# The first block of a two-block fp32 network on one core: a depthwise convolution accumulated in PSUM banks, VectorE's order within an attention step, a layer norm in five pieces, and two gate chunks spread over three steps

## The reference

```
h = rmsnorm(x, norm_g);  proj = h @ w_in            # (512, 1024) @ (1024, 3584)
y_a = silu(layernorm(depthwise_conv31(a_u * sigmoid(a_v)) + b)) * silu(a_z)
y_b = b_b * depthwise_conv3(b_c * b_x) * silu(b_z)
y_c = window_gqa(rope(c_q), rope(c_k), c_v, sink) * silu(c_z)     # 4 heads, band of 128
y_d = neighborhood_attn(d_q, d_k, d_v, bias) * silu(d_z)          # 4 heads, 8 x 64 grid
x = x + concat(y_a, y_b, y_c, y_d) @ w_out
```

## Time and profile before

| | us |
|---|---|
| median of 3 | 2107.06 (2106.79 to 2108.96) |
| the profiled execution | 2103.85 |
| its span in the profile | 2102.0 |
| granted TensorE clock over the span | 0.973 of full |
| first block, layers 0 and 1 | about 0 to 318 and 318 to 612 |

### The profile page before, as it was taken

The page is one execution under the profiler, slowest core; times in us unless marked ns, Lnnn a source line. Parts: engine busy times, 40 slices in busy tenths (PEclk is TensorE's granted clock), DMA queues, the critical chain, the costliest instruction groups (busy, mean ns, idle before and its releaser), DMA issues.

```text
span 2102.0 us, 25400 instructions
## 1 busy us (share of the span) xinstructions
PE 1970.2 (94%) x9140; PEld 1627.9 (77%) x9140; DVE 1184.4 (56%) x2109; ACT 745.4 (35%) x1079; POOL 1041.1 (50%) x1299
## 2 busy tenths in 40 slices
PE   6789799899789999899989999999998999999997
PEld 5677678677678888788878888778886888888886
DVE  7886658876566666646433233756666453332335
ACT  3333434334332545432413223324554224132230
POOL 5434245434264345556546464643446565574653
PEclk9899999999899999999999999999999999999998
DMA  4112122112122122222222222222212222222221
GB/s 168 67 67 71 61 74 97 62 65 81 33 78 95 66 81 81 80 100 82 105 80 101 100 96 88 98 80 81 81 61 94 89 99 100 94 89 98 100 101 60
DMA packets 28049, 178.85 MB, mean 85 GB/s; under 512 B 3872, under 2 KB 4000, under 8 KB 7456
## 3 DMA queue, kind: packets, MB, share of 16 engines
q1 hardware_dynamic: 24192, 169.88, 22.6%
q10 hardware_dynamic: 3744, 7.45, 1.1%
HBM read 175.22 MB, written 2.10 MB: 84 GB/s over the span
## 4 chain that ended last, share of the span: by engine, by line
issue 41%; POOL 35%; PE 23%; DVE 0%; POOLq 0%; DVEq 0%; ACT 0%
POOL W_lo L476 35%; PE bank L496 22%; DVE X L1945 0%; POOLq L480 0%; PE bank L544 0%; POOLq L473 0%; PE bank L537 0%; POOL SPARES L467 0%; DVE TMP L1507 0%; DVE PRE L1590 0%; DVE PR L1593 0%; DVE X L2315 0%; DVE PR L2312 0%; DVEq L169 0%; POOLq L476 0%
## 5 line engine op out<-in xcount | busy, mean ns | idle before, releaser
L476 POOL TENSOR_TENSOR W_lo<-W_raw,W_hi 128x256 fp32r<-128x256 f32 x1280 | 1039.3, 850 | 1024.3 <-ACT W_hi L1045 1024.0
L496 PE MATMUL bank<-H_hi,W_hi 128*128 128x512 f32 x1280 | 511.7, 400 | 13.4 <-POOL W_lo L476 11.0
L496 PE MATMUL bank<-H_hi,W_lo 128*128 128x512 f32 x1280 | 503.3, 393 | 0.0
L496 PE MATMUL bank<-H_lo,W_hi 128*128 128x512 f32 x1280 | 502.5, 393 | 0.0
L496 PE MATMUL bank<-Y_hi,W_hi 128*128 128x512 f32 x964 | 386.1, 401 | 22.2 <-POOL W_lo L476 11.4
L496 PE MATMUL bank<-Y_lo,W_hi 128*128 128x512 f32 x964 | 381.2, 395 | 0.0
L496 PE MATMUL bank<-Y_hi,W_lo 128*128 128x512 f32 x964 | 380.6, 395 | 0.0
L1045 ACT ACTIVATE W_hi<-W_raw 128x2048 fp32r<-128x2048 f32 x160 | 305.1, 1907 | 197.1 <-DMA W_raw<-in_stream 196.7
L496 PEld LDWEIGHTS bank<-H_hi,W_hi 128*128 128x128 f32 x1280 | 243.4, 190 | 68.0 <-POOL W_lo L476 15.4
L496 PEld LDWEIGHTS bank<-H_hi,W_lo 128*128 128x128 f32 x1280 | 242.8, 190 | 52.3
L496 PEld LDWEIGHTS bank<-H_lo,W_hi 128*128 128x128 f32 x1280 | 243.7, 190 | 48.6
...
## 6 DMA issues: line engine op xcount, KB each, us to landing
...
```

Of the source, the lines that this page charges most:

```text
L476: ins = nc.gpsimd.tensor_tensor(W[1][:, s, part], W_raw[:, s, part], W[0][:, s, part].bitcast(F32), ALU.subtract)
L496: mm = pe.matmul(out, lhs[a], rhs[b], start=(not begun and k == 0 and a == 0 and b == 0), stop=(not more and k == n - 1 and a == 1), skip_ ...
```

## The change

Four edits, all in the first block:

1. `conv_a` does channel tile 0 first and then tile 1, accumulating in a PSUM bank (`OB`, then `NB`); the last tap writes to `CA`. A tap waits for the tap just before. `FIRST_TAPS` becomes 6, 4, 7, 6, 2 and a new 6 ahead of `values(0)`, so that tile 0 is complete before attend(0) needs `OB`; steps 1 to 7 take the 31 taps of tile 1, in three places of each step.
2. VectorE's order in a step: `PT_lo` and the maximum come first, `lo_y(i-1)` after the maximum, and y(i) before the filler chunk's products (but in step 0). ScalarE takes the high part of y(i) before that of the merged gate, and waits for a freed bank before the next tanh rather than after its own.
3. The layer norm starts one step later (`LN_STEP` 7) and is cut into pieces that stand at three places of steps 8 to 12 (`norm_step`); its sum of squares on TensorE comes after attend(9), its spread in step 10, and the tanh goes into `HA` rather than `TMP`.
4. az0 and az1 are computed in steps 11, 12 and 13 (5, 3 + 2 and 6 k-tiles, `PARTS`), and o00 does k-tiles 0 and 1 last of its part.

```diff
-LN_STEP = 6
+LN_STEP = 7
 FILL = {0: "dz0", 1: "dz1", 2: "bc0", 3: "bc1", 4: "bx0", 5: "bx1", 6: "bb0", 7: "bb1",
-        8: "cz1", 9: "bz0", 10: "bz1", 11: "az0", 12: "az1", 14: "o00", 15: "o01"}
+        8: "cz1", 9: "bz0", 10: "bz1", 12: "az0", 13: "az1", 14: "o00", 15: "o01"}
+PARTS = {11: (("az0", 0, 5),), 12: (("az0", 5, 8), ("az1", 0, 2)), 13: (("az1", 2, 8),)}
-FIRST_TAPS = (15, 5, 6, 5, 2)
-TAPS = {0: 5, 1: 5, 2: 6, 3: 6, 4: 3, 5: 2, 6: 2}
+FIRST_TAPS = (6, 4, 7, 6, 2, 6)
+TAPS = {1: (1, 3, 2), 2: (1, 3, 2), 3: (1, 3, 2), 4: (1, 1, 1), 5: (1, 1, 1), 6: (1, 3, 1), 7: (1, 1, 0)}
...
+                for piece in PARTS.get(i, ()):
+                    part(*piece)
+                if i in FILL and i not in PARTS:
                     chunk(FILL[i])
...
-            taps = iter([(j, c) for j in range(CONV_A) for c in range(2)])
+            taps = iter([(j, c) for c in range(2) for j in range(CONV_A)])
...
+                    acc = (OB, NB)[c][:, :]
+                    dve.wait_ge(*own.last(0))
                     if j == 0:
-                        dve.wait_ge(*own.last(1))
-                        nc.vector.tensor_scalar(CA[:, c, :], src, w, par("conv_a_b", c), ALU.mult, ALU.add) \
-                            .then_inc(dve_step, own.step())
+                        ins = nc.vector.tensor_scalar(acc, src, w, par("conv_a_b", c), ALU.mult, ALU.add)
                     else:
-                        dve.wait_ge(*own.last(1))
-                        nc.vector.scalar_tensor_tensor(CA[:, c, :], src, w, CA[:, c, :], ALU.mult, ALU.add) \
-                            .then_inc(dve_step, own.step())
+                        ins = nc.vector.scalar_tensor_tensor(acc if j < CONV_A - 1 else CA[:, c, :], src, w, acc,
+                                                             ALU.mult, ALU.add)
+                    ins.then_inc(dve_step, own.step())
...
+            conv_a(FIRST_TAPS[5])
             values(0)
+            def norm_step(i, turn):
+                if (i, turn) == (LN_STEP + 1, "end"):
+                    dve.wait_ge(b1.ss.sem, b1.ss.at(l, "mean"))
...
+                elif (i, turn) == (LN_STEP + 2, "exp"):
...
+                elif (i, turn) == (LN_STEP + 2, "probs"):
...
+                elif (i, turn) == (LN_STEP + 3, "exp"):
+                    diagonals(b1, l, "var", spread=False)
+                elif (i, turn) in ((LN_STEP + 3, "end"), (LN_STEP + 4, "exp")):
+                    c = i - (LN_STEP + 3)
+                    dve.wait_ge(b1.bc.sem, b1.bc.at(l, "var"))
...
+                elif i == LN_STEP + 5 and turn != "end":
+                    c = ("exp", "probs").index(turn)
+                    dve.wait_ge(b1.aux.sem, b1.aux.at(l, f"ln{c}"))
...
             for i in range(2 * STEPS):
-                if i:
-                    lo_y(i - 1)
...
-                n_taps = TAPS.get(i, 0)
+                n_taps = TAPS.get(i, (0, 0, 0))
                 if i % STEPS < STEPS - 1:
                     softmax_max(i + 1)
-                    conv_a(n_taps // 4)
-                    n_taps -= n_taps // 4
+                if i % STEPS:
+                    lo_y(i - 1)
+                conv_a(n_taps[0])
+                norm_step(i, "exp")
+                if i % STEPS < STEPS - 1:
                     softmax_rest(i + 1)
-                conv_a(n_taps)
+                conv_a(n_taps[1])
+                norm_step(i, "probs")
...
                 nc.vector.scalar_tensor_tensor(PRE[r, i % 2, 0:256], OB[of:of + HD, 0:256], 0.5, ZB[r, h // 2,
                                                half * 256:(half + 1) * 256], ALU.mult, ALU.mult) \
                     .then_inc(b1.pre.sem, own.event(b1.pre, l, f"y{i}"))
...
+                if i in FILL and i:
+                    chunk(FILL[i])
+                norm_step(i, "end")
+                if i != LN_STEP:
+                    conv_a(n_taps[2])
```

More of the change, by code:

```diff
@@ L136, in b1_splits @@
         if i == STEPS:
-            out += ["cq0", "cq1", "ck0", "ck1", "cv"]
+            out += [f"y{i - 1}"] * low + ["cq0", "cq1", "ck0", "ck1", "cv"]
         if i == 1:
@@ L140, in b1_splits @@
         out += [f"pt{i}a"] if i < STEPS else [f"pt{i}a", f"pt{i}b"]
+        if low and i % STEPS:
+            out.append(f"y{i - 1}")
+        if not low:
+            out.append(f"y{i}")
         fill = FILL.get(i, "")
-        if i == LN_STEP + 4:
-            out.append("y" + FILL[i - 1])
-        if fill[:2] in ("bz", "az") and i != LN_STEP + 3:
+        if fill[:2] in ("bz", "az"):
             out.append("y" + fill)
-        out.append(f"y{i}")
-    return out
+    return out + [f"y{2 * STEPS - 1}"] * low
 def filled(name):
@@ L672, in chunk, with part @@
                 mm.then_inc(b1.done.sem, 1)
+            def part(name, first, last):
+                n = B1_CHUNKS.index(name)
+                k, c = divmod(n, 2)
+                if first == 0:
+                    if c == 0:
+                        begin_unit(1, l, k)
+                    free_bank(n)
+                pairs = chunk_pairs(slot_of(1, l, k), c, NORMED)[first:last]
+                mm = three(pe, b1_bank(name)[:, :], pairs, begun=first > 0, more=last < KT)
+                if last == KT:
+                    mm.then_inc(b1.done.sem, 1)
             def scores(i):
@@ L1128, in begin, with chunk @@
                 prep(1, l, k)
-            def chunk(name, begun=False):
+            def chunk(name, begun=False, last=True):
                 if not begun:
@@ L1150, in chunk @@
                 elif kind in ("dz", "cz", "bz", "az"):
+                    if name in ("dz1", "cz0", "cz1", "bz0"):
+                        act.wait_ge(b1.free.sem, b1.free.at(l, {"dz1": "dz0", "cz0": "dz1", "cz1": "cz0",
+                                                                "bz0": "cz1"}[name]))
                     act.wait_ge(*own.last(1))
```

124 lines of the change are left out of this document (54 added, 70 removed).

## The result

The changed kernel takes **2070.8 us** (median of 4, 2069.5 to 2071.8) against 2106.9 for the kernel before (median of 4, 2105.9 to 2109.0): a ratio of 0.983 with a 95% interval of 0.981 to 0.984, so 36.2 us won. The forecast was 2067.4, with a range of 2055 to 2085. Sign and range held; the terms of the sum did not all hold, and the errors went both ways.

A forecast was written before the change was run, and what follows sets the result against it. TensorE, busy 94%, was taken as the bound, its waits largely on a late VectorE. Terms of 49.7 us less 10 for the clock took 2103.85 to 2064.2, plus 3.2 for the median: 2067.4, range 2055 to 2085.

The forecast's parts named there:

- First attend: Up to the first attend: earlier split of dk1 cuts TensorE's wait; 11.3 us won in layer 0, 8.4 in layer 1.
- The price of the new tap: VectorE's convolution tap on a PSUM bank: 0.78 us whatever GpSimd does, bounds 0.68 and 1.37.
- Steps 0 to 7: Neighbourhood attention: VectorE still sets the stretch, 61.8 us instead of 71.3, 9.5 won in each layer.
- Between: Projections between the attention halves: from 1.9 us lost to 1.4 won, taken as 0.
- Last stretch: Window attention, steps 9 to 15: 65.2 us instead of 70.2 and 71.2, 5.0 and 6.0 won.
- the charge for the clock: Half-clock loss set against the gains: 4 us per last stretch, 1 per stretch of steps 0 to 7, 10 in all.
- The new stall at the spread: Step 10: the norm's diagonals come at 10.6 us after attend(9), TensorE wants them at 7.2; a 3.4 us stall.
- A: Whole program as summed: 2067.4 us, own range 2058 to 2077; chance 0.56.
- Rival D: Taps on a bank are still held up by GpSimd at 1.08 us: 15 us less won, 2083; chance 0.08.
- E: Slower than before: a tap reading and writing the same bank takes 1.37 us, 2137 in all; chance 0.04.
- C: Stalls too short to bring the clock down: 50 us won, 2057; chance 0.09.
- B: Five-piece norm costs more, step 10's stall drops the clock, the final stretch wins nothing: 2078 us; chance 0.20.

The follow-up runs named there:

- e1: Changed kernel with the convolution's accumulator back in SBUF, a tap still waiting for the one just before: 2078.7 us.
- e2: Kernel before with only the places of the taps changed (6, 4, 7, 6, 2 and 6 ahead, 31 in steps 1 to 6): 2101.4 us.
- e4: Changed kernel with 29 of the 31 taps of each channel tile left out, so the convolution is not computed: 2046.2 us.
- e3: Changed kernel with az0 and az1 whole in steps 12 and 13 and none in step 11: 2071.2 us.
- e7: Changed kernel with the next step's row maximum ahead of PT_lo in steps 8 to 14: 2059.7 us.
- e9: Changed kernel with the row maximum ahead of PT_lo in steps 8 to 14 and the merged gate's split a step later: 2052.8 us.
- e5: Changed kernel with the low half of y ahead of PT_lo again from the second step on: 2075.1 us.

## Why the prediction was right, and where it was not

**First attend: right.** 11.3 and 8.4 won by the forecast, 9.9 and 8.1 measured. dk1's split ended at 75.7 for 74.9 forecast (the taps began 0.5 us later than I took), and the wait ahead of the first scores was 1.6 for 1.2; layer 1 has none. The price of the new tap, 0.78, was exact. That VectorE's serial wait and not the bank makes it 0.78 and not 0.69 is shown by e1's and e2's rows with GpSimd idle. The price of the old tap I had read wrongly at its lower end: of the 13 taps in 12.09 us the last ones ran with GpSimd idle (it works from 57.7 to 66.4 there), so 0.92 is a mix of 0.69 and some 1.1, and not a tap beside GpSimd.

**Steps 0 to 7: the mis-sized term.** 9.5 won a layer by the forecast (8.5 with the clock), 4.2 and 4.3 measured. I took each step as the longer of VectorE's list and TensorE's 8.05 us. In step 5 my 9.2 us for VectorE was about right, as its rows in the changed kernel show: `PT_lo` starts at 136.47 and the next at 146.20, 9.7 us apart. The step takes 12.1 on TensorE, from attend(5) at 137.21 to attend(6) at 149.33.

```profile
136.47 0.68 DVE L1504 TENSOR_TENSOR PT_lo<-bank,PT_hi 128x512 fp32r<-128x512 f32 x1
137.07 1.36 DVE L1706 SCALAR_TENSOR_TENSOR BT<-BT,NM 128x640 f32<-128x640 f32 x1
141.12 0.58 DVE L1645 TENSOR_SCALAR PR<-PR,SM 128x192 f32<-128x192 f32 x2
146.20 0.68 DVE L1504 TENSOR_TENSOR PT_lo<-bank,PT_hi 128x512 fp32r<-128x512 f32 x1
```

The matmuls of TensorE's chunk in that step, the second and third, and two after its middle:

```profile
142.72 0.63 PE L498 MATMUL bank<-Y_lo,W_hi 128*128 128x512 f32 x1
143.15 0.63 PE L498 MATMUL bank<-Y_hi,W_lo 128*128 128x512 f32 x1
...
145.90 0.39 PE L498 MATMUL bank<-Y_hi,W_hi 128*128 128x512 f32 x1
146.13 0.40 PE L498 MATMUL bank<-Y_lo,W_hi 128*128 128x512 f32 x1
```

From `PT_lo` to the probabilities VectorE needs 5.2 us, and TensorE has only attend and scores to do meanwhile: it waits 0.98 and 1.24 us (rows of its waits, above). Only then does its chunk begin, which is 5.6 us of work that nothing in VectorE's list can shorten. And behind that wait it starts at the lower level, 1.2 GHz: its matmuls begin 0.43 us apart, and 0.23 later; the first eight take 3.5 us in place of 1.8. So in a step with a long chain the two engines run partly in series: the step is VectorE's chain plus TensorE's chunk, and the maximum of two sums is only a lower bound. Steps 1, 3 and 5 hold nearly all of it: from attend to attend they take 11.4, 9.1 and 12.1 us in the changed kernel and 7.6, 7.9 and 7.6 in e4. From attend(0) to attend(7) TensorE stands for 5.1 us and is busy for 60.3 where e4 has 55.5, with the same matmuls; together they are the 10 between 65.4 and 55.5. Of the 4.8 us more of busy time the clock costs 3.4 (1.7 in each of steps 1 and 5, at a mean of 0.85 and 0.86; in step 3, behind a wait of 1.09, it is 1.00); the other 1.4 these rows don't explain. The bias operation had part in it, 1.05 to 1.36 us in the steps for the 0.8 to 0.9 I took.

**Between: right.** 0 by the forecast, 0.6 won.

**Last stretch: the chain right, the charge for the clock too large.** 5.0 and 6.0 less 4 for the clock by the forecast; 3.8 and 4.7 measured. Counted as I counted, attend(11) to attend(14) of layer 0 come 6.8, 16.8, 25.1 and 34.7 us after attend(10), for 7.0, 16.6, 25.1 and 34.7 in the sum. Step 9 took 8.0 as forecast, step 10 11.7 for 12.5, and o00's last piece came at 46.5 for 44.7. The new stall at the spread was to be 3.4 us and is 0.61: the diagonals were ready 1.1 us sooner after attend(9) than I summed, and TensorE came to them 1.8 us later, since I had left out its sums of squares behind attend(9) and their wait (206.38 [0.88]). The other waits are 1.3 to 2.1 us at the transposes, as named. The clock did not fall more than before: it is 0.95 over this stretch in both layers, where it was 0.93 and 0.88. In layer 0 matmuls begin 0.43 us apart twice, from 228.3 to 230.8 and from 255.2 to 258.1. The first costs nothing at the end: e4 has none there, and its attend(13) and attend(14) come just as long after attend(10) (25.1 and 34.8), since VectorE's chain sets them. The second stands behind the last wait at the transposes, where TensorE waits no more for that chain, and is nearly all of the 1.8 us by which o00's last piece is late: from attend(14) to attend(15) the changed kernel takes 10.2 us, and layer 1 of e4, which has no such stretch there, 8.4. So the clock took some 1.8 us from the sum in layer 0 and not 4. And the credit that I gave to the spread az chunks is refuted by e3: taking them back costs nothing. That the stretch is set by the chain from `PT_lo` over the maximum and the exponentials to `PR`, and by the merged split ahead of it, was in my list of steps, but I didn't see that most of it need not stand there; e7 to e9 show it, with 9 us a layer.

**Sum.** The forecast won 39.7 and the chip 36.2, because 8.5 us too much in steps 0 to 7 and 1.7 in the first stretches met 5.5 us too little in the last ones and 1.2 between. That the total came within 3.4 us of the forecast is luck for the greater part: 10.2 us too much and 6.7 too little cancelled. (The chances of A to D add up to 0.93, where the prediction says 0.92.) Rival D is refuted by the 0.78 beside GpSimd, E by the same rows, C by the clock of 0.95, and B by the last stretches, which did win.

**Two rules beside the rows.** Four serial taps take 3.13 us on a bank and 3.12 in SBUF, with GpSimd idle. The Trainium skill, VectorE: DVE Perf Modes, section on the TRN2 errata, would have an operation from PSUM to SBUF take some 65 ns more than one from SBUF to SBUF; these taps write the bank as well as read it. For this form the measurement decides: no difference. The last tap of a tile, which reads the bank and writes `CA`, takes 0.75 us (at 88.71). And beside GpSimd a tap takes 0.78 us on a bank and 1.03 to 1.14 in SBUF, GpSimd's eight products 5.6 and 8.7. The Trainium skill, SBUF — State Buffer, section on the two separate sides, has VectorE with two SBUF inputs and GpSimd shut each other out for a whole instruction. The trace agrees on who is slowed and who is not. That it is for the whole instruction these rows don't show: in the third group of e1 the 6 taps beside GpSimd take 1.07 us each and its products 1.09, less than the 0.78 and 0.70 that each takes alone would make one after the other.

**What each part brought**, as far as the runs tell: the bank 8 us against serial taps in SBUF (e1), the order of y 4 (e5), the pieces of az nothing (e3), the places of the taps alone 5 to 7 in the kernel before (e2). That is half of the 36, if these add up, which was not tried. The other parts (y ahead of the chunk, the taps in three turns of a step, ScalarE's later wait for a freed bank, the norm in pieces) were not run one by one, nor was the bank against the old alternating taps, and how the other half divides among them stays open.
